# Two edits in a gated recurrence: the keys' transposes half a unit later, and the sums of squares as two split products

## The chip, the cores and the metric

The kernel runs on one core of a Trainium2 chip. The metric is the device time of one launch in microseconds (us). Three runs of the kernel before gave 2029.32, 2033.02 and 2034.14 us, so the median is 2033.02.

## The reference, cut to what matters

Two blocks follow each other, both on 1024 tokens of width 1024. The first one holds the stage that is changed: a recurrence of eight heads with 128 keys and 128 values each. Of one head it computes

```
z = h @ w_in                      # four of its parts: q, f_pre, i_in (the values v), g_h
f = lb + (1 - lb) * sigmoid(f_pre);   log_f = log(f);   k = 1 - f
o = recurrence(q, log_f, k, v)    # state <- decay * state + k_dec^T v, in chunks, causal
o = rms_norm(o, hgrn_norm_w) * silu(g_h)      # rms over the 128 values of the head
```

Everything is float32. Where the kernel needs float32 accuracy from TensorE it splits a matrix x into a rounded part hi (type fp32r) and the rest lo = x - hi, and adds the products of the parts.

## The kernel before, in words

**The stages.** After the first norm come the input projection with the recurrence, the pooling groups, the output projection, and then the second block. The recurrence lies between about 87 and 615 us of the profiled execution.

**The projection's units.** A unit is 128 columns of w_in over all tokens. A half unit (`fm_half`) is 8 x 3 matmuls of 128x512: for each k the three split products (lines 1003 to 1005). A head has four units, j = 0 for the forget gate, 1 for the output gate, 2 for the values, 3 for the queries. Units alternate between PSUM slots 0 and 1. The matmuls of unit 4 * it + j are for head it, while the tasks put between the half units are those of head h = it - 1. `head(h, z)` writes that order out by hand for TensorE:

```
z(0, 0)   task_o(h - 1)      z(0, 1)   task_ms(h - 1)
z(1, 0)   task_t0(h)   task_t1(h)      z(1, 1)   task_base(h)   task_span(h, 0)
z(2, 0)   task_span(h, 1)   task_u(h)  z(2, 1)   task_span(h, 2)
z(3, 0)   task_span(h, 3)    z(3, 1)   task_span(h, 4)
```

**The tasks.** `task_t0` (line 1131) transposes the values into PSUM slot 2 and `task_t1` (line 1140) the decayed keys into slot 3, eight transposes each. ScalarE copies both out (`take_vk`, through the copy helper at line 1693). `task_base` (line 1148, sixteen matmul records) multiplies keys and queries within blocks of 4. `task_span(h, j)` (line 1164) does it between the halves of blocks of 128, 64, 32, 16 and 8; spans 0 and 1 wait for the copied keys, since they write the banks of slot 3. `task_o` (lines 1181, 1183) makes the output of the head before in slot 3, and `task_ms` (line 1190) sums its squares over the partitions by a product with a matrix of ones, 128x512 for each half, into slot 2. Plain float32 matmuls show as two records each.

**ScalarE of a head** (`begin` and `step`): base exponentials (lines 1799, 1800), exponentials of spans 0 and 1 (line 1794), squares of the last output (line 1853), the exponential for the queries (line 1842), sigmoid of the forget gate (line 1807), `o_norm` with a Ln (line 1858) and an Exp (line 1860) that end in 1 / rms, then `take_vk`, the exponential of span 2, the output gate's sigmoid (line 1811), spans 3 and 4. An ACT_TABLE_LOAD stands ahead of most changes of function.

**VectorE of a head** (`spans`): base differences (lines 2562, 2565), differences of spans 0 and 1 (lines 2556, 2557), the products of keys and queries with the base exponentials (lines 2570, 2571), with those of span 0 (lines 2578, 2579), with the decayed queries (line 2632), then `back_3(h - 1)`, which waits for 1 / rms and scales the last head's output out of PSUM slot 3 (line 2656, after which `task_t1` may write that slot) and multiplies by the gate (line 2660), then the products of span 1, the differences of span 2, and the picks out of PSUM.

**GpSimd** rounds and splits the weights of each unit: line 795 makes w_hi, line 798 w_lo, 128x1024 each. The work for unit u starts when TensorE has finished unit u - 2 (the loop waits for `w_used` of 4 * i + s - 1). In four of the loop's turns it also makes sums of the output projection's weights (`t_sum_ahead`, line 822): one behind the first unit, one behind the second, two behind the third, none behind the fourth. SyncE's queue loads the weights ahead of all that.

Of the kernel before, what the change touches and what calls it, by code (L numbers as in the profile page):

```python
# [25 lines left out]
F32 = mybir.dt.float32  # L26
F32R = mybir.dt.float32r
I32 = mybir.dt.int32
ACT = mybir.ActivationFunctionType
ALU = mybir.AluOpType  # L30
# [190 lines left out]
def program(nc, ap):  # L221
    ctx = ExitStack()
    with ctx:
        def sb(name, shape, dt=F32):
            return ctx.enter_context(nc.sbuf_tensor(name, shape, dt))
# [15 lines left out]
        arena = sb("arena", [P, 27 * PAGE])  # L241
        arena_at = nc.sbuf_base - 27 * PAGE * 4
        ident = sb("ident", [P, P])
        ones = sb("ones", [P, P])
        cols = sb("cols", [P, VROWS])
        lvl_mask = sb("lvl_mask", [P, P + NL * 64], I32)
        st = sb("st", [P, 160])
# [10 lines left out]
        def page(i, n=1):  # L258
            return arena[:, i * PAGE:(i + n) * PAGE]
# [4 lines left out]
        def two_banks(slot):  # L264
            return psum[:, 2 * slot:2 * slot + 2, :].rearrange("p b n -> p (b n)")
# [53 lines left out]
        first_hi, first_lo = [first_[:, :, e, :] for e in range(2)]  # L319
        first_raw = page(FIRST_RAW, 2).rearrange("p (u c) -> p u c", c=PAGE)  # L320
        first_raw_k = lambda s: (first_raw if s < 2 else w_raw)[:, s, :].rearrange("p (k c) -> p k c", c=P)
        gate_part = [page(GATE_W)[:, h * HALF:(h + 1) * HALF] for h in range(2)]
        acc_mm = psum[:, X_BANKS, P:P + 2 * KT]
        gate_row = page(GATE_ROW)
# [672 lines left out]
        def _(pe):  # L997
# [127 lines left out]
            def task_t0(h):  # L1125

                pe.wait_ge(vt_done, h + 1)
                if not (type(h) is int and h == 0):
                    pe.wait_ge(ln_done, h)
                for i in range(NT):  # L1130
                    mm = pe.transpose(blocks128(two_banks(2), i), blocks128(page(B_VT), i), ident[:])
                mm.then_inc(task_full, 1)

            def task_t1(h):

                pe.wait_ge(kdec_done, h + 1)
                if not (type(h) is int and h == 0):
                    pe.wait_ge(o1_done, h)
                for i in range(NT):
                    mm = pe.transpose(blocks128(two_banks(3), i), blocks128(page(B_KDT), i), ident[:])  # L1140
                mm.then_inc(task_full, 1)
# [43 lines left out]

            def task_ms(h):

                pe.wait_ge(sq_done, h + 1)
                for half in range(2):
                    mm = pe.matmul(psum[:, 4 + half, :], ones[:], page(B_SQ)[:, half * HALF:(half + 1) * HALF], start=True, stop=True)  # L1190
                mm.then_inc(task_full, 1)

            def head(h, z):

                first = type(h) is int and h == 0
                z(0, 0)
                if not first:
                    task_o(h - 1)
                z(0, 1)
                if not first:  # L1200
                    task_ms(h - 1)
                z(1, 0)
                task_t0(h)
                task_t1(h)
                z(1, 1)
                task_base(h)
                task_span(h, 0)
                z(2, 0)
                task_span(h, 1)
                task_u(h)  # L1210
                z(2, 1)
                task_span(h, 2)
                z(3, 0)
                task_span(h, 3)
                z(3, 1)
                task_span(h, 4)
# [472 lines left out]
        def _(act):  # L1689
            A = act.activation  # L1690

            def copy(out, in_):
                return A(out, in_, ACT.Copy)  # L1693
# [98 lines left out]
            def span_exp(h, j):  # L1792
                act.wait_ge(d_done, NL * h + j + 1)
                A(page(B_D[j % 3]), page(B_D[j % 3]), ACT.Exp).then_inc(e_done, 1)

            def base_exp(h):

                act.wait_ge(d4_done, h + 1)
                A(page(B_K4), page(B_Q4), ACT.Exp, scale=-1.0).then_inc(e4_done, 1)
                A(page(B_Q4), page(B_Q4), ACT.Exp).then_inc(e4_done, 1)  # L1800
# [8 lines left out]
            def gate_sig(it):  # L1809
                act.wait_ge(w_used, 4 * it + 2)  # L1810
                A(mix_slot(it), two_banks(1), ACT.Sigmoid).then_inc(gsig_done, 1)
# [22 lines left out]
            def begin(h):  # L1834

                base_exp(h)
                span_exp(h, 0)
                span_exp(h, 1)
                if not (type(h) is int and h == 0):
                    o_squares(h - 1)  # L1840
                act.wait_ge(b_done, h + 1)
                A(qe, bB, ACT.Exp).then_inc(eb_done, 1)

            def take_vk(h):

                act.wait_ge(task_full, TASKS * h + 1)
                copy(page(B_V), two_banks(2)).then_inc(v_done, 1)
                act.wait_ge(task_full, TASKS * h + 2)
                copy(page(B_KD), two_banks(3)).then_inc(kd_done, 1)

            def o_squares(h):
                act.wait_ge(task_full, TASKS * h + TASK_O)
                A(page(B_SQ), two_banks(3), ACT.Square).then_inc(sq_done, 1)

            def o_norm(h):
# [17 lines left out]
            def step(it):  # L1873

                h = it - 1
                begin(h)
                front(it, 4 * it)
                if not (type(it) is int and it == 1):
                    o_norm(h - 1)
                take_vk(h)  # L1880
                span_exp(h, 2)
                gate_sig(it)
                span_exp(h, 3)
                span_exp(h, 4)
                take_v(it, 4 * it)
                log_f(it)
                take_q(it, 4 * it)
                decays(it)
# [6 lines left out]
            def pool_in(g, j):  # L1895
# [5 lines left out]
                else:  # L1901
# [5 lines left out]
            act.wait_ge(fc_done, HEADS)  # L1907
            pool_in(0, 0)
            o_norm(h - 1)
            take_vk(h)  # L1910
            act.dma_start(page(PW[0]).rearrange("p (g c d) -> p g c d", g=2, c=2),
                          ap["pool_w"][0, 0:2].rearrange("g (c p) d -> p g c d", p=P)).then_inc(pw_in, 16)
            span_exp(h, 2)
            pool_in(0, 1)
            span_exp(h, 3)
            span_exp(h, 4)
# [460 lines left out]
        def _(dve):  # L2377
# [186 lines left out]
                ref = page(B_K4)[:, 0:S // BASE].rearrange("p (n a) -> p n a", a=1).to_broadcast([P, S // BASE, BASE])  # L2564
                STT(x.rearrange("p (n w) -> p n w", w=BASE), ref, -0.5, b4, ALU.mult, ALU.add).then_inc(d4_done, 1)

            def base_kq(h):

                dve.wait_ge(e4_done, 2 * h + 2)
                TT(page(B_K4), page(B_K4), kk_, ALU.mult).then_inc(kq4_done, 1)  # L2570
                TT(page(B_Q4), page(B_Q4), qq, ALU.mult).then_inc(kq4_done, 1)

            def span_kq(h, j):
# [35 lines left out]
            def states(h):  # L2609
# [4 lines left out]
                for c in range(NT - 1):  # L2614
# [3 lines left out]
                    else:  # L2618
                        dve.wait_ge(s_done, (NT - 1) * h + c)
                        STT(sst[:, c * P:(c + 1) * P], sst[:, (c - 1) * P:c * P], end_decay[:, c:c + 1], u, ALU.mult, ALU.add).then_inc(s_done, 1)  # L2620

            def spans(h, gate, f):

                at = [(TASKS * h + SPAN_TASK[j], NL * h + j if j else h + 1) for j in range(NL)]
                base_d(h)
                span_d(h, 0)
                span_d(h, 1)
                dve.wait_ge(q_done, h + 1)
                base_kq(h)
                span_kq(h, 0)  # L2630
                dve.wait_ge(eb_done, h + 1)
                TT(qe, qe, qq, ALU.mult).then_inc(qe_done, 1)
                if not (type(h) is int and h == 0):
                    back_3(h - 1)
                span_kq(h, 1)
                span_d(h, 2)
                base_pick(h)
                span_kq(h, 2)
                pick(h, 0, at)
                span_d(h, 3)  # L2640
                gate()
                pick(h, 1, at)
                span_d(h, 4)
                states(h)
                span_kq(h, 3)
                span_kq(h, 4)
                pick(h, 2, at)
                f()
                pick(h, 3, at)
                pick(h, 4, at)  # L2650
# [41 lines left out]
            def window(g, c):  # L2692

                dve.wait_ge(pu_done, 2 * g + c + 1)
                u = page(U_PAGES[g % 2][c])
                src, w = u, 1
                for a in range(G_ORDER[g] + 1):
                    dst = page((S_A, S_B)[a % 2])
                    dve.tensor_copy(dst[:, 0:w], src[:, 0:w]).then_inc(win_step, 1)
                    steps[0] += 1  # L2700
                    wstep(TT(dst[:, w:S], src[:, w:S], src[:, 0:S - w], ALU.add))
                    src, w = dst, 2 * w
                dve.wait_ge(rc_in, 16)
                wstep(TT(src[:, 0:w], src[:, 0:w], page(RC)[:, 16 * G_ORDER[g]:16 * G_ORDER[g] + w], ALU.mult))
                TT(u[:, 0:w], src[:, 0:w], u[:, 0:w], ALU.subtract).then_inc(win_step, 1)
                steps[0] += 1
                STT(u[:, w:S], src[:, w:S], 1.0 / w, u[:, w:S], ALU.mult, ALU.subtract).then_inc(pd_done, 1)
                dve.wait_ge(pd_done, 2 * g + c + 1)
# [29 lines left out]
            spans(h, lambda: pool_gate(0, 0), lambda: pool_gate(0, 1))  # L2738
            dve.wait_ge(task_full, TASKS * h + TASK_O)
            window(0, 0)  # L2740
            window(0, 1)
            back_3(h)
            pool_gate(1, 0)
# [787 lines left out]
```

## Time and profile before

| | |
|---|---|
| median of three runs | 2033.02 us (2029.32 to 2034.14) |
| the profiled execution | 2031.16 us, of which the span is 2029.2 us |
| PE busy | 1973.9 us, 97% |
| DVE / ACT / POOL busy | 1352.0 (67%) / 824.5 (41%) / 941.1 us (46%) |
| the chain that ended last | PE 80%, DVE 10%, ACT 5%, issue 3% |
| mean granted TensorE clock | 0.992 of full speed |

PE is TensorE, DVE VectorE, ACT ScalarE, POOL GpSimd. The span runs from the first to the last instruction; the 2 us around it are the launch. The share of PE is an average over all stages. "Idle before" in a row is the time that the engine sat idle just before those instructions, with what ended it. Times in the timelines are microseconds from the start of the span: start, then duration. Matmuls overlap, so their cost in a stream is the distance from start to start.

### The profile page before, as it was taken

The page shows a single profiled execution, that of the slowest core. Times are in us where ns is not written, and L with a number is a line of the kernel's source. Part 1 is how long each engine was busy: PE and PEld are TensorE (multiplying, and loading weights), DVE is VectorE, ACT ScalarE, POOL GpSimd, SP SyncE. Part 2 cuts the span into 40 slices and gives each one's busy share as a digit, 9 for nine tenths or more (in the row PEclk, how much of TensorE's full clock was granted, in tenths as well). Part 3 has the DMA queues.
Part 4 walks back from the last instruction along what each step waited for, and adds up shares of the span by engine and source line. Part 5 has one row for each costly group of instructions (what it writes and reads, how often), then busy time and mean ns, then how long its engine had stood idle before and what let it go on. Part 6 is the DMA issues. An engine that isn't in the chain of part 4 may idle for free.

```text
span 2029.2 us, 27449 instructions
## 1 busy us (share of the span) xinstructions
PE 1973.9 (97%) x10053; PEld 1623.2 (80%) x10053; DVE 1352.0 (67%) x1784; ACT 824.5 (41%) x1313; POOL 941.1 (46%) x548
## 2 busy tenths in 40 slices
PE   7999999999999999999999899898999999999997
PEld 6888888888887768878888678776888888888886
DVE  7887777666536754687061487798856656667978
ACT  5444444344411014463200476657323323334443
POOL 1354454422324459753354110855755455445553
PEclk8999999999999999999999899999999999999999
DMA  9223222211122244044110200222423323357344
GB/s 285 75 81 117 73 72 103 84 40 31 42 63 58 68 156 135 11 177 126 42 51 11 84 2 1 73 104 80 139 88 109 114 88 109 103 183 242 104 137 164
DMA packets 179501, 193.98 MB, mean 96 GB/s; under 512 B 9863, under 2 KB 122968, under 8 KB 179418
## 3 DMA queue, kind: packets, MB, share of 16 engines
q1 hardware_dynamic: 172996, 178.53, 27.8%
q10 hardware_dynamic: 6422, 14.37, 2.0%
q8 instruction: 49, 0.80, 0.2%
q14 instruction: 34, 0.28, 0.0%
HBM read 151.71 MB, written 41.16 MB: 95 GB/s over the span
## 4 chain that ended last, share of the span: by engine, by line
PE 80%; DVE 10%; ACT 5%; issue 3%; POOL 1%; ACTq 0%; DVEq 0%; POOLq 0%
PE psum L1003 7%; PE psum L1558 7%; PE psum L1560 7%; PE psum L1559 7%; PE psum L1005 6%; PE psum L1004 6%; PE psum L1164 3%; PE psum L1661 3%; PE psum L1662 3%; PE psum L1663 3%; PE psum L1024 3%; PE psum L1025 3%; PE psum L1023 3%; PE psum L1319 2%; PE psum L1321 2%
## 5 line engine op out<-in xcount | busy, mean ns | idle before, releaser
L795 POOL TENSOR_TENSOR w_hi<-w_raw,ones 128x1024 fp32r<-128x1024 f32 x60 | 149.2, 2487 | 481.8 <-PE psum L1005 357.5
L1003 PE MATMUL psum<-h_hi,w_hi 128*128 128x512 f32 x704 | 284.2, 404 | 0.0
L1005 PE MATMUL psum<-h_hi,w_lo 128*128 128x512 f32 x704 | 274.8, 390 | 0.0
L1004 PE MATMUL psum<-h_lo,w_hi 128*128 128x512 f32 x704 | 274.2, 389 | 0.0
L798 POOL TENSOR_TENSOR w_lo<-w_raw,w_hi 128x1024 fp32r<-128x1024 f32 x60 | 166.7, 2779 | 4.7
L1693 ACT ACTIVATE arena<-psum 128x1024 f32<-128x1024 f32 (+7 forms) x103 | 80.3, 787 | 216.4 <-PE psum L1005 136.0
L1003 PEld LDWEIGHTS psum<-h_hi,w_hi 128*128 128x128 f32 x704 | 132.3, 188 | 28.5 <-issue 2.6
L1004 PEld LDWEIGHTS psum<-h_lo,w_hi 128*128 128x128 f32 x704 | 132.4, 188 | 28.3 <-issue 2.6
L1005 PEld LDWEIGHTS psum<-h_hi,w_lo 128*128 128x128 f32 x704 | 132.1, 188 | 28.4
L1661 PE MATMUL psum<-w_hi,h_hi 128*128 128x512 f32 x308 | 120.8, 392 | 3.1 <-DVE h_lo L3294 3.1
L993 POOL TENSOR_TENSOR w_lo<-arena,w_hi 128x512 fp32r<-128x512 f32 x61 | 86.3, 1419 | 75.5 <-ACT w_hi L1693 75.5
L1662 PE MATMUL psum<-w_lo,h_hi 128*128 128x512 f32 x308 | 120.5, 391 | 0.0
L1663 PE MATMUL psum<-w_hi,h_lo 128*128 128x512 f32 x308 | 120.4, 391 | 0.0
L1693 ACT ACTIVATE w_hi<-arena 128x512 fp32r<-128x512 f32 (+1 forms) x111 | 66.1, 605 | 83.7 <-DVE arena L3270 69.1
L1023 PE MATMUL psum<-w_hi,h_hi 128*128 128x512 f32 x256 | 99.6, 389 | 0.0
L1024 PE MATMUL psum<-w_lo,h_hi 128*128 128x512 f32 x256 | 99.6, 389 | 0.0
L1025 PE MATMUL psum<-w_hi,h_lo 128*128 128x512 f32 x256 | 99.6, 389 | 0.0
L1558 PE MATMUL psum<-h_hi,w_hi 128*128 128x512 f32 x252 | 98.2, 390 | 0.0
L1560 PE MATMUL psum<-h_hi,w_lo 128*128 128x512 f32 x252 | 98.1, 389 | 0.0
L1559 PE MATMUL psum<-h_lo,w_hi 128*128 128x512 f32 x252 | 98.0, 389 | 0.0
L984 POOL TENSOR_TENSOR w_lo<-w_raw,w_hi 128x512 fp32r<-128x512 f32 x40 | 64.6, 1616 | 63.2 <-ACT w_hi L1693 63.2
L3294 DVE TENSOR_TENSOR h_lo<-arena,h_hi 128x512 fp32r<-128x512 f32 x77 | 66.3, 867 | 35.3 <-ACT h_hi L1693 35.0
(489 smaller groups left out, 5227.5 us busy)
## 6 DMA issues: line engine op xcount, KB each, us to landing
w_raw<-w_in SPq DMA_DIRECT2D x64, 512.0 KB, 3.8
act_op<-arena SPq DMA_DIRECT2D x77, 256.0 KB, 2.3
arena<-act_op SPq DMA_DIRECT2D x77, 256.0 KB, 2.7
w_raw<-w_gate SPq DMA_DIRECT2D x22, 512.0 KB, 4.1
w_raw<-w_up SPq DMA_DIRECT2D x22, 512.0 KB, 5.2
arena<-ada_w SPq DMA_DIRECT2D x16, 512.0 KB, 7.2
arena<-w_out SPq DMA_DIRECT2D x16, 512.0 KB, 5.6
out_T<-arena SPq DMA_DIRECT2D x16, 512.0 KB, 5.8
```

Of the source, the lines that this page charges most:

```text
L798: pool.tensor_tensor(w_lo[:, c, :], raw, w_hi[:, c, :].bitcast(F32), ALU.subtract).then_inc(w_ready, 1)
L1003: pe.matmul(o, wh, xh, start=(k == 0), stop=False)
L1004: pe.matmul(o, wh, xl, start=False, stop=False)
L1005: return pe.matmul(o, wl, xh, start=False, stop=(k == KT - 1))
L1023: pe.matmul(psum[:, t, :], xh, wh, start=start, stop=False)
L1024: pe.matmul(psum[:, t, :], xh, wl, start=False, stop=False)
L1558: pe.matmul(o, wh[:, at], xh, start=(k == 0), stop=False)
L1559: pe.matmul(o, wh[:, at], xl, start=False, stop=False)
L1560: return pe.matmul(o, wl[:, at], xh, start=False, stop=(k == 3))
L1661: pe.matmul(o, ah, bh, start=(j == 0), stop=False)
L1662: pe.matmul(o, ah, bl, start=False, stop=False)
L1663: return pe.matmul(o, al, bh, start=False, stop=(j == DJ - 1))
```

## The change

It does three things. `task_t1` goes behind `z(1, 1)`, just ahead of `task_base`, on TensorE. ScalarE's `take_vk` is cut in two, and the copy of the keys goes behind the exponential of span 2. The sum of squares is split: ScalarE squares the output twice out of PSUM, once rounded to fp32r (page 5, one of the pages of the spans' differences) and once in full (page 7); VectorE subtracts one from the other in place; TensorE multiplies both with ones of type fp32r. ScalarE's squares go ahead of the exponentials of spans 0 and 1, and VectorE's subtraction between the two base products. No DMA changes its place, except that the load of the pooling weights in the last head stays behind the copy of the keys, and this copy is later.

```diff
-        ones = sb("ones", [P, P])
+        ones_r = sb("ones_r", [P, P], F32R)
+        ones = ones_r[:].bitcast(F32)
...
+        sq_hi, sq_lo = [rounded_pages(name, i, 1)[:] for name, i in (("sq_hi", B_D[2]), ("sq_lo", B_SQ))]
...
             def task_ms(h):
-                pe.wait_ge(sq_done, h + 1)
-                for half in range(2):
-                    mm = pe.matmul(psum[:, 4 + half, :], ones[:], page(B_SQ)[:, half * HALF:(half + 1) * HALF], start=True, stop=True)
+                for e, sq in enumerate((sq_hi, sq_lo)):
+                    pe.wait_ge(sq_done, 3 * h + (2 + e))
+                    for half in range(2):
+                        mm = pe.matmul(psum[:, 4 + half, :], ones_r[:], sq[:, half * HALF:(half + 1) * HALF], start=(e == 0), stop=(e == 1))
                 mm.then_inc(task_full, 1)
...
                 task_t0(h)
+                z(1, 1)
                 task_t1(h)
-                z(1, 1)
                 task_base(h)
...
             def begin(h):
                 base_exp(h)
+                if not (type(h) is int and h == 0):
+                    o_squares(h - 1)
                 span_exp(h, 0)
                 span_exp(h, 1)
-                if not (type(h) is int and h == 0):
-                    o_squares(h - 1)
...
             def o_squares(h):
                 act.wait_ge(task_full, TASKS * h + TASK_O)
+                A(sq_hi, two_banks(3), ACT.Square).then_inc(sq_done, 1)
                 A(page(B_SQ), two_banks(3), ACT.Square).then_inc(sq_done, 1)
...
-                take_vk(h)
+                take_vt(h)
                 span_exp(h, 2)
+                take_kd(h)
                 gate_sig(it)
...
+            def squares_lo(h):
+                dve.wait_ge(sq_done, 3 * h + 2)
+                TT(sq_lo, page(B_SQ), sq_hi.bitcast(F32), ALU.subtract).then_inc(sq_done, 1)
...
-                base_kq(h)
+                base_k(h)
+                if not (type(h) is int and h == 0):
+                    squares_lo(h - 1)
+                base_q(h)
                 span_kq(h, 0)
...
             window(0, 0)
+            squares_lo(h)
             window(0, 1)
```

`base_k` and `base_q` are the two instructions of `base_kq`. `take_vt` and `take_kd` are the two halves of `take_vk`, each with its own wait for TensorE.

## Rows read from the trace of the kernel before

**Rows 1.** The page's first part: busy time, share and instructions of each engine.
```profile
PE 1973.9 (97%) x10053; PEld 1623.2 (80%) x10053; DVE 1352.0 (67%) x1784; ACT 824.5 (41%) x1313; POOL 941.1 (46%) x548
```

**Rows 2.** PE's timeline in the fourth head: start, us, line, operation, count, idle before.
```profile
350.50 1.93 PE L1190 MATMUL psum<-arena,ones 128*128 128x512 f32 x4
...
357.76 1.03 PE L1131 MATMUL psum<-ident,arena 128*128 128x128 f32 x8
359.85 1.06 PE L1140 MATMUL psum<-ident,arena 128*128 128x128 f32 x8 [1.05 <-DVE arena L2656]
366.23 1.95 PE L1148 MATMUL psum<-arena 128*128 128x128 f32 x16
368.10 1.15 PE L1164 MATMUL psum<-arena 128*64 128x64 f32 x16
```

**Rows 3.** PE's timeline in the fifth head, where nothing waits.
```profile
414.21 1.88 PE L1190 MATMUL psum<-arena,ones 128*128 128x512 f32 x4
...
421.42 1.04 PE L1131 MATMUL psum<-ident,arena 128*128 128x128 f32 x8
422.29 1.04 PE L1140 MATMUL psum<-ident,arena 128*128 128x128 f32 x8
```

**Rows 4.** PE's timeline: fourth and last matmul of one half unit, twenty steps apart.
```profile
336.90 0.39 PE L1003 MATMUL psum<-h_hi,w_hi 128*128 128x512 f32 x1
...
341.43 0.39 PE L1005 MATMUL psum<-h_hi,w_lo 128*128 128x512 f32 x1
```

**Rows 5.** ACT's timeline in the fourth head.
```profile
349.39 1.01 ACT L1853 ACTIVATE arena<-psum 128x1024 f32<-128x1024 f32 x1
350.30 1.04 ACT L1842 ACTIVATE arena<-arena 128x1024 f32<-128x1024 f32 x1
...
365.33 1.06 ACT L1794 ACTIVATE arena<-arena 128x1024 f32<-128x1024 f32 x1 [3.35 <-DVE arena L2557]
```

**Rows 6.** DVE's timeline in the fourth head, and its line 2660 in the fifth.
```profile
351.37 3.38 DVE L2632 TENSOR_TENSOR arena<-arena 128x1024 f32<-128x1024 f32 x1
358.42 1.28 DVE L2656 SCALAR_TENSOR_TENSOR arena<-psum,cols,arena 128x1024 f32<-128x1024 f32 x1 [3.67 <-ACT arena L1860]
359.74 3.15 DVE L2660 TENSOR_TENSOR arena<-arena 128x1024 f32<-128x1024 f32 x1
...
364.62 0.68 DVE L2557 TENSOR_TENSOR arena<-arena 128x512 f32<-128x512 f32 x1
...
421.49 1.22 DVE L2660 TENSOR_TENSOR arena<-arena 128x1024 f32<-128x1024 f32 x1
```

**Rows 7.** POOL's timeline in the fourth head.
```profile
350.74 2.92 POOL L795 TENSOR_TENSOR w_hi<-w_raw,ones 128x1024 fp32r<-128x1024 f32 x1 [6.96 <-PE psum L1005]
...
356.97 4.83 POOL L822 TENSOR_TENSOR arena<-arena 128x1024 f32<-128x1024 f32 x2
366.47 2.35 POOL L795 TENSOR_TENSOR w_hi<-w_raw,ones 128x1024 fp32r<-128x1024 f32 x1 [4.66 <-PE psum L1005]
```

**Rows 8.** The timeline of POOL and DVE in the first head.
```profile
110.53 4.69 POOL L795 TENSOR_TENSOR w_hi<-w_raw,ones 128x1024 fp32r<-128x1024 f32 x1 [6.93 <-PE psum L1005]
...
115.29 2.72 POOL L798 TENSOR_TENSOR w_lo<-w_raw,w_hi 128x1024 fp32r<-128x1024 f32 x1
115.69 2.88 DVE L2579 TENSOR_TENSOR arena<-arena 128x512 f32<-128x512 f32 x1
```

**Rows 9.** The timeline of DVE and PE in the first head.
```profile
112.28 0.69 DVE L2557 TENSOR_TENSOR arena<-arena 128x512 f32<-128x512 f32 x1
...
113.28 1.15 PE L1164 MATMUL psum<-arena 128*64 128x64 f32 x16
```

**Rows 10.** PE's waits, 10 to 55 us: waited for, us in total, times, longest.
```profile
PE psum L1088 <- DVE arena L2467: 7.7, 1, 7.7
```

**Rows 11.** PE by microsecond at that wait: stretch, length, busy, granted clock.
```profile
32.00:33.00 1.00, 0.00 (x0) 0.58 1.18 288
...
39.00:40.00 1.00, 1.00 (x6) 1.00 1.19 298
```

More of the change, by code:

```diff
@@ L1836, in begin, with take_vt, take_kd @@
                 base_exp(h)
+                if not (type(h) is int and h == 0):
+                    o_squares(h - 1)
                 span_exp(h, 0)
                 span_exp(h, 1)
-                if not (type(h) is int and h == 0):
-                    o_squares(h - 1)
                 act.wait_ge(b_done, h + 1)
                 A(qe, bB, ACT.Exp).then_inc(eb_done, 1)
-            def take_vk(h):
+            def take_vt(h):
                 act.wait_ge(task_full, TASKS * h + 1)
                 copy(page(B_V), two_banks(2)).then_inc(v_done, 1)
+            def take_kd(h):
                 act.wait_ge(task_full, TASKS * h + 2)
@@ L1909, in _ @@
             o_norm(h - 1)
-            take_vk(h)
+            take_vt(h)
+            span_exp(h, 2)
+            take_kd(h)
             act.dma_start(page(PW[0]).rearrange("p (g c d) -> p g c d", g=2, c=2),
                           ap["pool_w"][0, 0:2].rearrange("g (c p) d -> p g c d", p=P)).then_inc(pw_in, 16)
-            span_exp(h, 2)
             pool_in(0, 1)
@@ L2565, in base_d, with base_k, base_q @@
                 STT(x.rearrange("p (n w) -> p n w", w=BASE), ref, -0.5, b4, ALU.mult, ALU.add).then_inc(d4_done, 1)
-            def base_kq(h):
+            def base_k(h):
                 dve.wait_ge(e4_done, 2 * h + 2)
                 TT(page(B_K4), page(B_K4), kk_, ALU.mult).then_inc(kq4_done, 1)
+            def base_q(h):
                 TT(page(B_Q4), page(B_Q4), qq, ALU.mult).then_inc(kq4_done, 1)
```

## The prediction

> **What bounds the kernel now.** I read the page first: TensorE is busy 97% of the span [rows 1], so an edit pays only where it shortens TensorE's stream or one of its few waits. Then the stream of one head. In the fourth head the values' transposes start at 357.76 and the keys' at 359.85 [rows 2]; undisturbed they are 0.87 apart [rows 3], so 1.22 us is lost, and the row blames VectorE's line 2656, which frees PSUM slot 3. Heads 1 to 4 show this wait (four rows alike), heads 5 to 7 none. The difference between them is GpSimd: in the fourth head it has two extra sums [rows 7], and VectorE's lines 2632 and 2660 stretch to 3.38 and 3.15 us, where line 2660 took 1.22 in the fifth head [rows 6]. They stretch because they wait for a GpSimd instruction to end: the two sums run from 356.97 to 361.80, and line 2660 ends at 362.89, one undisturbed length later. Line 2656, which reads PSUM, is not held (1.28).
>
> So the thing to follow is a chain beside TensorE: squares, 1 / rms, line 2656, line 2660, four half-page instructions, the exponential of span 2 at 365.33 [rows 5]. Today nothing on TensorE waits for that exponential before much later. After the change the keys' copy stands behind it on ScalarE, and `task_span(h, 0)` waits for that copy.
>
> **The change, part by part.**
>
> The products with ones. Today, in the fifth head, 7.21 us from their start to the next transposes [rows 3], less a half unit. Twenty steps of its matmuls take 4.53 us, 0.2265 each [rows 4], so 24 take 5.44 and the four float32 records 1.77. Four fp32r matmuls of the same width at 0.2265 are 0.91: 0.86 us less, in each of eight heads.
>
> The transposes. TensorE's work is the same; the wait of 1.22 goes from heads 1 to 4. What would be late next is the values' transposes, which wait for the Ln to leave slot 2, and then span 0.
>
> ScalarE. One more Square costs the distance between lines 1853 and 1842, 0.91 us [rows 5]. The squares lie ahead of everything up to 1 / rms, which moves from 358.4, where line 2656 waits for it [rows 6], to 359.3. The output is ready for them (`task_o` ends at 345). The copy of the keys, 1.03 us, moves behind the exponential.
>
> VectorE. The subtraction has the size of two half-page instructions, 1.2 us. It waits for the second square (349.45 by the shifted rows) and ends at 350.7, just before TensorE needs it after the two hi products (350.50 + 0.45): no wait there. VectorE then still has the base product of the queries, both span 0 products and line 2632 to do, 3.5 us, from 350.7 on. Until now only line 2632 was left at that moment.
>
> GpSimd's requests. Line 795 asks at 350.74 as before [rows 7], because z(0, 1) ends as before. Line 798 and the two sums follow, some 2.4 us each. The next line 795 asks when z(1, 1) ends. That was 366.23; now it is 357.0 (values' transposes, just held by the Ln) + 0.87 + 5.5 = 363.4, so it asks at 363.6 and not at 366.47. This is what the moved transposes trigger: two GpSimd instructions fall into the stretch in which VectorE has its last four short ones to do.
>
> How they share. At 115.69 a half-page VectorE instruction was issued while the one before it had itself been held; GpSimd, which had asked at 115.29, went first, and the VectorE one took 2.88 us for its 0.68 [rows 8]. So they alternate once both queue. The other bound is the first of these rows: GpSimd was kept for 2.3 us behind five VectorE instructions in a row that nothing had held (4.69 for 2.35). I work both out:
> - Alternating from 350.74: the queries' base product ends at 351.8, GpSimd 354.15, VectorE 354.75, GpSimd 357.1, VectorE 357.7, sum 360.05, line 2632 361.2, sum 363.55, line 2660 364.7 (line 2656 ran beside the sum), line 795 367.05, 367.65, line 798 370.0, then the last three short ones: 371.8.
> - VectorE first until it idles at 354.15: the four GpSimd instructions then run with line 2660 between the sums and the first short one behind them, and the chain ends at 371.95.
>
> Both end near 371.9, because from 350.7 on there are six GpSimd instructions (14.1) and VectorE's 7 us to fit in, with no hole left. Then come the exponential (1.06) and the copy (1.03): the keys are there at 374.1. TensorE, without that, would reach span 0 at 363.4 + 0.87 + 1.87 = 366.1. It stands 8.0 us, and span 0 starts 6.0 us later than the 368.10 of [rows 2]. This net already holds the two gains. Four heads: +24.0.
>
> The Trainium skill, page "SBUF — State Buffer", section "Who interferes with whom", says that a VectorE instruction with two SBUF inputs and a GpSimd one that reads SBUF exclude each other, the second to issue waiting out the first, and that one with at most one SBUF input is free. The rows of lines 2660 and 2656 agree with both halves. By the rule alone GpSimd would get in behind whatever VectorE runs when it asks, the first of my two orders; the row of 4.69 us bears out the second. The sum is the same to 0.2 us a head.
>
> The clock. TensorE has one long wait, 7.7 us [rows 10], from 27.5 to about 35.1. Before it the granted clock was full; it fell to half, 1.2 GHz, during the wait (0.58 between 32 and 33) and came back to 2.4 GHz only at 39 [rows 11]. Some 4.2 us of work ran at half speed: 2.1 us lost. A wait of 8.0 us should do the same. I take 2.1 for each of four: +8.4. The lower bound is 0; the upper is the whole half-clock stretch after the wait, about 6.8 us and so 3.4 lost.
>
> The first head. It has no squares. The base products there wait for the copied values anyway. VectorE's difference for span 2 ends at 112.97 [rows 9]; exponential and copy end at 115.1, and span 0 follows instead of 113.28: +1.8. If line 795 came first there, it would be +4.2.
>
> The later heads, 5 to 7. There is no extra sum. In the fifth head line 2660 starts at 421.49 now [rows 6] and, with the later 1 / rms, at 422.3 then; VectorE's short ones end 3.6 us later at 425.9, the exponential at 427.0. The keys' transposes end at 427.8 (421.42 - 0.86 + 0.87 + 5.5 + 0.87), so the copy waits for them and is done at 429.05, before TensorE's 429.7. Only the products' gain stays: three times 0.86, and once more for the eighth head's products during the pooling stage, where VectorE has the subtraction done long before: -3.4.
>
> The sum against the profiled execution's 2031.16: +24.0 + 8.4 + 1.8 - 3.4 = +30.8, so 2062.0. The median of the runs is 1.9 above that execution, within their spread of 4.8, and I leave it there. Everything behind the recurrence is again TensorE's and moves along.
>
> **The rivals.**
> 1. Only one GpSimd instruction gets between the short ones. Span 0 is then 3.5 us late, not 6.0 or 6.1: 2031.2 + 14.0 + 1.8 - 3.4 = 2043.6, or up to 2052 with the clock. For it: an unheld VectorE run kept GpSimd out once [rows 8]. Against: the run would have to begin unheld.
> 2. VectorE keeps its run together: the four short ones end at 367.0, the keys are there at 369.2, +1.1 a head: 2031.2 + 4.6 + 1.8 - 3.4 = 2034.2, no change that can be told.
> 3. The other side: the chain keeps ahead of TensorE in all heads, as in 5 to 7. Then 8 x 0.86 + 4 x 1.22 = 11.8 comes off: 2019.4. This decides where the keys are copied by 366.1. Unheld all the way, the chain would give 359.3 + 1.3 + 3.6 + 2.1 = 366.3, so it needs GpSimd to stay out of the way. For it: in the later heads the same chain is in time, and the order in which the two engines meet is worked out from shifts of tenths of a microsecond. Against: 14.1 us of GpSimd work has nowhere to go in that stretch.
> 4. The clock stays at half for longer, or the subtraction comes after line 795's request (its margin is 0.05 us) and holds the products with ones for about 3 us as well: up to 2074.
>
> **How the numbers follow.** My case has 0.42, rival 1 has 0.20, rival 2 has 0.13, rival 3 has 0.15, rival 4 has 0.10. The number is my case's, 2062.0; its own range, with the clock's bounds, is 2053 to 2068. With rivals 1 and 2 taken in, the range is 2032 to 2068; left out are the third and most of the fourth. A difference of 0.3%, 6 us, is about what a measurement of this kernel can tell from none: faster 0.15, within it 0.13, slower 0.72.
>
> **What would show it.** Right: in heads 1 to 4 the span 0 row of PE has an idle time of about 8 us released by ScalarE's copy; the second short instruction of line 2578 or 2579 before it takes about 2.9 us; the granted clock has four dips; the products with ones are four records at 0.23 apart; heads 5 to 7 show no wait. Wrong: no idle time before span 0 in the loop's first turns, or one of 1 us; or a wait before the products with ones.

## The result and the profile after

The changed kernel takes 2059.69 us (median of 4 runs, 2057.79 to 2060.74) against 2033.58 us: a ratio of 1.0134, with a 95% interval of 1.0122 to 1.0147. The profiled execution took 2059.16 us, 28.0 more than that of before. The forecast was 2062.0.

The page's first part, and the list of PE's longest wait in the recurrence (waited for, us in total, times, longest):

```profile
PE 1978.0 (96%) x10053; PEld 1631.9 (79%) x10053; DVE 1384.9 (67%) x1792; ACT 831.6 (40%) x1321; POOL 954.4 (46%) x548
```
```profile
PE psum L1166 <- ACT arena L1696: 28.3, 5, 6.7
```

Against [rows 1] TensorE's busy time grew by 4.1 us and its idle time in the span by 24.0. The idle time lies in five waits of span 0 (now line 1166) for ScalarE's copy, 28.3 us in all, where the kernel before had four waits of 1.05. Line numbers have moved. On TensorE 1133 and 1142 are the two transposes, 1150 the base products, 1193 the products with ones. On ScalarE 1696 is the copy and 1797 the spans' exponential. On VectorE 2636 is the subtraction, 2583 the queries' base product, 2590 and 2591 the spans' products, 2651 the decayed queries' product, 2675 and 2679 the old 2656 and 2660, and 2565 and 2566 the spans' differences. On GpSimd 797, 800 and 824 are the old 795, 798 and 822. PE's timeline in the fourth head, to be held against [rows 2]:

```profile
373.73 0.61 PE L1193 MATMUL psum<-sq_hi,ones_r 128*128 128x512 f32 x2
374.18 0.62 PE L1193 MATMUL psum<-sq_lo,ones_r 128*128 128x512 f32 x2
...
380.30 1.06 PE L1133 MATMUL psum<-ident,arena 128*128 128x128 f32 x8
386.69 1.04 PE L1142 MATMUL psum<-ident,arena 128*128 128x128 f32 x8
387.56 1.95 PE L1150 MATMUL psum<-arena 128*128 128x128 f32 x16
396.16 1.97 PE L1166 MATMUL psum<-arena 128*64 128x64 f32 x16 [6.64 <-ACT arena L1696]
```

Both intended gains are there. The products with ones take 0.90 us (the next half unit starts at 374.63), and the keys' transposes follow z(1, 1) with no wait. Then TensorE stands for 6.64 us, and the 16 records behind it take 1.97 us where they took 1.15: the granted clock is 0.50 from 395 to 401. ScalarE's timeline shows what came last:

```profile
394.06 1.06 ACT L1797 ACTIVATE arena<-arena 128x1024 f32<-128x1024 f32 x1 [10.61 <-DVE arena L2566]
395.02 1.01 ACT L1696 ACTIVATE arena<-psum 128x1024 f32<-128x1024 f32 x1
```

The keys' transposes were done at 387.7, but their copy stood behind an exponential that waited until 394.06 for VectorE. VectorE's timeline, with GpSimd's under it, shows why, against [rows 6, 7]:

```profile
372.67 1.23 DVE L2636 TENSOR_TENSOR sq_lo<-arena,sq_hi 128x1024 fp32r<-128x1024 f32 x1 [0.35 <-ACT arena L1860]
373.81 1.22 DVE L2583 TENSOR_TENSOR arena<-arena 128x1024 f32<-128x1024 f32 x1
374.94 2.90 DVE L2590 TENSOR_TENSOR arena<-arena 128x512 f32<-128x512 f32 x1
377.76 2.88 DVE L2591 TENSOR_TENSOR arena<-arena 128x512 f32<-128x512 f32 x1
380.56 3.41 DVE L2651 TENSOR_TENSOR arena<-arena 128x1024 f32<-128x1024 f32 x1
383.90 1.27 DVE L2675 SCALAR_TENSOR_TENSOR arena<-psum,cols,arena 128x1024 f32<-128x1024 f32 x1
385.20 2.11 DVE L2679 TENSOR_TENSOR arena<-arena 128x1024 f32<-128x1024 f32 x1
387.24 2.84 DVE L2590 TENSOR_TENSOR arena<-arena 128x512 f32<-128x512 f32 x1
390.00 2.82 DVE L2591 TENSOR_TENSOR arena<-arena 128x512 f32<-128x512 f32 x1
```
```profile
373.97 3.32 POOL L797 TENSOR_TENSOR w_hi<-w_raw,ones_r 128x1024 fp32r<-128x1024 f32 x1 [6.95 <-PE psum L1007]
377.37 2.72 POOL L800 TENSOR_TENSOR w_lo<-w_raw,w_hi 128x1024 fp32r<-128x1024 f32 x1
380.05 6.18 POOL L824 TENSOR_TENSOR arena<-arena 128x1024 f32<-128x1024 f32 x2
386.93 2.60 POOL L797 TENSOR_TENSOR w_hi<-w_raw,ones_r 128x1024 fp32r<-128x1024 f32 x1 [0.70 <-PE psum L1007]
389.61 2.67 POOL L800 TENSOR_TENSOR w_lo<-w_raw,w_hi 128x1024 fp32r<-128x1024 f32 x1
```

A half-page instruction of 0.68 us takes 2.8 to 2.9 in four places, each time with one GpSimd instruction inside, and lines 2651 and 2679 are held in the same way by the two sums; six GpSimd instructions lie between 373.97 and 392.28. Line 2675, which reads PSUM, is not held. In the fifth head, without the sums, nothing waits:

```profile
457.19 1.04 PE L1142 MATMUL psum<-ident,arena 128*128 128x128 f32 x8
458.06 1.95 PE L1150 MATMUL psum<-arena 128*128 128x128 f32 x16
459.94 1.15 PE L1166 MATMUL psum<-arena 128*64 128x64 f32 x16
```

The granted clock around the four waits, 25 us each (stretch, length, PE busy, clock, then the DMA's share and rate):

```profile
180.00:205.00 25.00, 21.35 (x117) 0.81 0.52 190
251.00:276.00 25.00, 21.16 (x115) 0.80 0.53 189
322.00:347.00 25.00, 20.74 (x120) 0.86 0.53 189
392.00:417.00 25.00, 20.84 (x116) 0.86 0.25 68
```

The clock has two levels here, full (2.4 GHz) and half (1.2 GHz), so 0.81 of 25 us means some 9.5 us at 1.2 GHz and 0.86 some 7, a part of it inside the wait.

### The profile page after: what moved, and what is told of

It reads as the page before. It is cut to its first block, busy times and chain, and to the rows that moved or that the text cites. A ratio compares the mean times of both kernels' runs of the same rounds, so it can differ in the third digit from the quotient of the medians.

```text
span 2057.3 us, 27477 instructions
## 1 busy us (share of the span) xinstructions
PE 1978.0 (96%) x10053; PEld 1631.9 (79%) x10053; DVE 1384.9 (67%) x1792; ACT 831.6 (40%) x1321; POOL 954.4 (46%) x548
## 4 chain that ended last, share of the span: by engine, by line
PE 78%; DVE 13%; ACT 4%; issue 3%; POOL 1%; ACTq 0%; DVEq 0%; POOLq 0%
PE psum L1561 6%; PE psum L1562 6%; PE psum L1563 6%; PE psum L1005 6%; PE psum L1007 6%; PE psum L1006 6%; PE psum L1166 3%; PE psum L1664 3%; PE psum L1666 3%; PE psum L1665 3%; PE psum L1026 3%; PE psum L1025 3%; PE psum L1027 3%; PE psum L1322 2%; PE psum L1324 2%
## 5 line engine op out<-in xcount | busy, mean ns | idle before, releaser
L797 POOL TENSOR_TENSOR w_hi<-w_raw,ones_r 128x1024 fp32r<-128x1024 f32 x60 | 156.2, 2603 | 497.2 <-PE psum L1007 373.0
L1166 PE MATMUL psum<-arena 128*128 128x64 f32 (+1 forms) x640 | 73.0, 271 | 28.3 <-ACT arena L1696 28.3
L1166 PEld LDWEIGHTS psum<-arena 128*128 128x128 f32 (+1 forms) x640 | 73.2, 189 | 32.1 <-issue 27.3
```

The lines of the kernel that those rows point to most:

```text
L1166: mm = pe.matmul(o, kq[:, 0:rows], late, start=True, stop=True)
```

## The experiments

Ten kernels, in three groups in the order below: four, four and two. The ones of a group ran on one chip, with the kernel before beside them (medians 2030.16, 2032.96 and 2032.79 us), so ratios are to that. "The port" in the expectations is what VectorE's instructions with two SBUF inputs and GpSimd's share, so that one holds the other.

**The copy put back ahead of the exponential.** In the loop and in the last head:

```diff
                 take_vt(h)
-                span_exp(h, 2)
                 take_kd(h)
+                span_exp(h, 2)
```

> The changed kernel with one swap on ScalarE: the copy of the keys goes back ahead of the exponential of span 2. Theory (the wait before span 0 comes from the copy standing behind an exponential that VectorE feeds late): the keys are there about 1.2 us after their transposes end, before the base products end, so the wait of 6.6 us and the four clock dips go away; both intended gains appear, 8 x 0.86 and 4 x 1.22 us: about 2031.2 - 11.8 = 2019 to 2022 us, faster than both kernels. Rival (the chain of VectorE and GpSimd decides whatever ScalarE's order is): the wait moves to another task of the same heads, span 1 or span 2 or the products with queries, and the time stays at 2045 or more. Second rival (the exponential of span 2 is now what is late): a wait of 1 to 4 us before span 2 in heads 1 to 4, 2025 to 2035.

Measured: 2020.77 us, ratio 0.9950 (0.9935 to 0.9964), faster than both kernels. PE's only wait between 95 and 660 us is one that the kernel before had too, in the first head:

```profile
PE psum L1150 <- ACT arena L1696: 0.9, 1, 0.9
```

So the whole loss came through the place of that one copy, and both rivals fall. The chain beside TensorE is as late as it was: the exponential of span 2 starts 20.39 us behind the head's products with ones (365.92 against 345.53), in the changed kernel 20.33. But nothing that TensorE needs soon stands behind it, and the wait did not move to span 1 or 2.

**The transposes alone.** The changed kernel with the sums of squares as before (one Square behind the exponentials of spans 0 and 1, float32 products, no subtraction).

> Only the keys' transposes and their copy moved, sums of squares as before. Theory: GpSimd's next request comes at 364.4 on the clock of the kernel before, when VectorE is already in its unheld run of four short instructions (362.8 to 365.3) and keeps the port; the exponential ends at 366.4, the copy at 367.4, span 0 starts 0.6 us earlier than before in heads 1 to 4 after an idle time of about 0.6 us, too short for the clock to fall; first head +1.8 us. Sum about -0.6: 2030 to 2034 us. Rival (the moved transposes alone bring the collision): two GpSimd instructions in between, span 0 starts 4 us late, 2045 to 2055 us.

Measured: 2047.11 us (2040.17 to 2049.99), ratio 1.0082 (1.0065 to 1.0099). The theory was wrong here. The rival had the sign and the range, but with two GpSimd instructions in between, and there is one. In the profiled execution, of 2040.17 us, span 0 waits 2.7 us in each of the four heads. The rows of DVE and POOL:

```profile
370.23 0.68 DVE L2562 TENSOR_TENSOR arena<-arena 128x512 f32<-128x512 f32 x1
...
370.83 2.84 DVE L2563 TENSOR_TENSOR arena<-arena 128x512 f32<-128x512 f32 x1
```
```profile
370.53 2.59 POOL L796 TENSOR_TENSOR w_hi<-w_raw,ones 128x1024 fp32r<-128x1024 f32 x1 [2.50 <-PE psum L1006]
```

VectorE was in its third short instruction of an unheld run, and GpSimd went in ahead of the fourth. I had expected the run to keep GpSimd out. One GpSimd instruction in between is 2.2 us, so the first three heads took 65.2 us each and not 63.1. The fourth took 66.8, and there alone the granted clock fell behind the wait:

```profile
375.00:400.00 25.00, 24.20 (x134) 0.93 0.25 66
```

So after a wait of 2.7 us the clock fell in one head of this execution and not in the three before, at a price of 1.6 us. The three executions of 2046 to 2050 us had a lower mean clock (0.986 to 0.988) than the profiled one (0.990). It is an estimate that it fell in more of their heads: 0.003 of 2047 us is 6 us of clock, about 12 us at the lower level, which cost 6 us. That is most of the difference.

**The squares alone.** Transposes side by side again, both copies ahead of the exponential of span 2, squares split.

> Only the sums of squares split; the transposes of values and keys stand together and both copies ahead of the exponential of span 2, as before. Theory: in heads 1 to 4 VectorE comes to line 2656 of the kernel before some 2 to 3.5 us later, because the subtraction pushes three instructions behind GpSimd's request and they alternate; the keys' transposes wait for it 3 to 5 us instead of 1.2. The products save 0.86 in each of eight heads. Sum: 4 x (2 to 3.5) - 6.9 = +1 to +7: 2032 to 2040 us. Rival (the subtraction is hidden, the squares are harmless): 2031.2 - 6.9 + 4 x 0.9 (1 / rms later by a Square) = 2028 us.

Measured: 2047.69 us, ratio 1.0086 (1.0066 to 1.0105): worse than the theory's range. The wait before the keys' transposes is as expected, the granted clock behind it is not. The waits of the loop and the row of the fourth head:

```profile
PE psum L1142 <- DVE arena L2675: 17.1, 6, 3.9
```
```profile
376.41 1.94 PE L1142 MATMUL psum<-ident,arena 128*128 128x128 f32 x8 [3.91 <-DVE arena L2675]
```

Eight transposes take 1.94 us instead of 1.04: half the clock, in each of the four heads (mean clock 0.88 to 0.90 in 25 us there). I had left the clock out of that sum. A head took 68.4 us for 63.7: 2.85 more of waiting, 0.87 less of products, and the 2.7 that are left fit the clock (0.10 to 0.12 of 25 us is 2.5 to 3.0). The four heads make 18.7 us, and the profiled execution (2047.54) is 16.4 above 2031.16; the rest of the program took 2.3 less.

**The two sums moved.** The changed kernel with

```diff
-                    for name in (["T3"], ["T2"], ["T1", "T4"], [])[s]:
+                    for name in (["T3"], ["T2"], [], ["T1", "T4"])[s]:
```

> The changed kernel, with GpSimd's two sums of a loop turn behind the fourth unit instead of the third, so that they are not in the queue between the products with ones and span 0. Theory (the port between VectorE and GpSimd makes the chain late): VectorE's instructions wait for 2 GpSimd instructions fewer, span 0 of heads 1 to 4 starts about 4 to 5 us earlier, an idle time of 0 to 3 us is left, and the clock mostly stays full: 2031 to 2042 us. Rival (the extra Square, the subtraction and the copy's new place make the chain late without GpSimd): no change against the changed kernel, 2055 to 2060 us.

Measured: 2023.49 us, ratio 0.9964 (0.9950 to 0.9977). All four waits are gone; only the first head's, 1.7 us, is left:

```profile
PE psum L1166 <- ACT arena L1696: 1.7, 1, 1.7
```

This took more off than I had expected. With two GpSimd instructions in the first group and not four, VectorE began its last short instruction at 360.93 on that execution's clock, just ahead of GpSimd's next request at 361.03. So it is not two instructions that drop out but four: the second group falls behind the whole run, by a margin of 0.1 us. Nothing was changed on ScalarE, so the extra Square and the copy's new place are harmless once GpSimd's instructions are out of the way.

**The same move in the kernel before (control).**

> The kernel before, with GpSimd's two sums of a loop turn behind the fourth unit instead of the third. Control for the runs that move these sums. Theory (the wait of 1.2 us before the keys' transposes in heads 1 to 4 comes from VectorE being held by GpSimd's instructions ahead of line 2656): it goes away, 4 x 1.2 us: about 2025 to 2027 us. Rival (it comes from ScalarE's chain to 1 / rms alone): no change.

Measured: 2031.64 us, ratio 0.9997 (0.9987 to 1.0006): no change. The wait before the keys' transposes stays as in [rows 2]:

```profile
PE psum L1140 <- DVE arena L2656: 4.2, 4, 1.1
```

So the gain above is not one of moving the sums as such. And the theory was wrong on where that wait comes from; a later run settles it. [rows 6] could have told as much: behind line 2632 VectorE sits idle for 3.67 us until ScalarE's 1 / rms is there, so the hold of line 2632 delays nothing, and line 2660 comes behind line 2656.

**The squares alone, with the sums moved.**

> Only the sums of squares split, and the sums behind the fourth unit. Theory (the loss of the squares alone, 3.9 us of waiting before the keys' transposes and the half clock behind it, comes from the port and not from the extra Square): 1 / rms is 0.9 us later than in the kernel before, so a wait of 0.5 to 1.5 us before the keys' transposes is left in up to seven heads, and 0.86 comes off in eight: 2022 to 2028 us. Rival (the subtraction and the Square are too long by themselves): the wait stays above 3 us and the time above 2040.

Measured: 2035.43 us, ratio 1.0016 (1.0007 to 1.0026). Between the two statements. The four long waits fall from 3.9 to 2.6 us, not to 0.5 to 1.5:

```profile
PE psum L1142 <- DVE arena L2675: 11.9, 6, 2.6
```

What is left is, by my estimate, the 1.05 us of before, 0.9 from the second Square and 0.86 because TensorE arrives sooner by the shorter products, 2.8 in all; I had left the last out. The 1.3 us that went are the share of the two sums. The granted clock fell behind the first of these waits (eight transposes in 1.94 us) and not behind the other three (1.06 us).

**The transposes alone, with the copy ahead.**

> Only the keys' transposes moved, with the copy of the keys ahead of the exponential of span 2. Theory: the wait of 1.2 us in heads 1 to 4 is all that the move can save, 4.9 us: 2025 to 2027 us, so the split products account for the other 5 to 7 us of the 2020.8 of the version with both. Rival (the move by itself also lets GpSimd start earlier and shortens more): 2021 to 2023 us, and the split products give next to nothing.

Measured: 2026.70 us, ratio 0.9974 (0.9964 to 0.9983). Heads 1 to 6 take 62.4 us each. This is as expected, and it splits the gain: 5 to 6 us for the move, and the rest of the 10 us of the version with both for the products with ones. In the profiled executions the last products with ones start at 612.27 us before, 606.99 with the move and 602.78 with both. From there to the end the three take 1416.9, 1416.7 and 1415.8 us.

**The wait filled.** The changed kernel with work thrown away in heads 1 to 6:

```diff
                 task_base(h)
+                if type(h) is not int:
+                    pe.wait_ge(sig_done, h + 2)
+                    for _ in range(28):
+                        pe.matmul(psum[:, 0, :], ones_r[:], h_hi[:, 0, 0:HALF], start=True, stop=True)
                 task_span(h, 0)
```

> The changed kernel, with 28 matmuls of ones by a slice of h_hi (128x512, fp32r, 6.3 us, into a PSUM slot whose content has been taken) between the base products and span 0 in the loop's heads 1 to 6. They only keep TensorE busy; their product is thrown away. Theory (the half clock behind the wait costs TensorE 1.7 to 3.4 us in each of heads 1 to 4): span 0 starts at the same distance from the head's start as without them, the granted clock stays full there, and each of heads 1 to 4 gets shorter by 2 to 3.5 us (70.7 us from one products with ones to the next becomes 67.5 to 69); heads 5 and 6 get 6 us longer. Sum: 2059 - 8 to -14 + 12 = 2057 to 2063 us. Rival (the clock costs nothing, the wait is all): heads 1 to 4 keep 70.7 us, 2070 us.

Measured: 2062.48 us, ratio 1.0146 (1.0130 to 1.0163). PE's timeline in the fourth head, and the granted clock there:

```profile
381.66 1.95 PE L1150 MATMUL psum<-arena 128*128 128x128 f32 x16
383.37 6.60 PE L1213 MATMUL psum<-h_hi,ones_r 128*128 128x512 f32 x28
```
```profile
387.00:412.00 25.00, 24.63 (x144) 1.00 0.24 63
```

The clock stays full in all four. The slow heads take 68.6 us each (299.25 to 367.83 between products with ones) instead of 71.2, 71.4, 69.9 and 70.8: 1.3 to 2.8 us less, 2.2 on average, at the same distance from base products to span 0 (8.67 against 8.60). Two heads are longer by 6.4. So the half clock behind the wait is worth 2.2 us a head on average, and the rival falls.

**The single sum moved, kernel before.** The order is now `(["T3"], [], ["T2"], ["T1", "T4"])`: the single sum goes behind the third unit, and the two of the third behind the fourth, which alone had changed nothing.

> The kernel before, with the single sum that stands behind the second unit put behind the third, and the two of the third behind the fourth. Moving the two alone left the wait before the keys' transposes as it was. Theory (that wait comes from the single sum: it holds VectorE's base differences for 2.2 us in heads 1 to 4, so that the whole chain to 1 / rms is 2.2 us later than in heads 5 to 7): the wait of 1.2 us goes away in the four heads, 62.4 us a head instead of 63.7, about 2031 - 5 = 2026 us. Rival (something else in these turns holds it, the transfers of the sums' operands for example): 63.7 us a head stay.

Measured: 2026.38 us, ratio 0.9971 (0.9960 to 0.9981). The wait is gone, and a head takes 62.4 us. DVE's line 2562 in the fourth head, first in the kernel before, then in this one:

```profile
341.50 2.79 DVE L2562 TENSOR_TENSOR arena<-arena 128x256 f32<-128x256 f32 x1
```
```profile
338.35 0.60 DVE L2562 TENSOR_TENSOR arena<-arena 128x256 f32<-128x256 f32 x1
```

PE's two groups of transposes stand 0.87 apart:

```profile
354.56 1.03 PE L1131 MATMUL psum<-ident,arena 128*128 128x128 f32 x8
355.43 1.04 PE L1140 MATMUL psum<-ident,arena 128*128 128x128 f32 x8
```

The 1.2 us were lost some 15 us ahead of where the wait shows (341.50 to 344.29, against 358.80).

**No subtraction.** The changed kernel without `squares_lo` and the lo product; its sums are those of the rounded squares alone.

> The changed kernel without VectorE's subtraction and without the product of the lo part (the sums of squares are those of the rounded squares alone); both Squares stay on ScalarE. Theory (the number of GpSimd instructions that come between decides, and they stay six): worked out from the changed kernel's rows, the last short instruction ends 0.6 us earlier, TensorE comes to span 0 0.46 us earlier, so the wait there stays at 6.0 to 6.6 us in heads 1 to 4; with 8 x 0.45 us of products less the time is 2053 to 2057 us. Rival (the subtraction is what makes the chain late, since without it and the second Square the wait was 2.7 us): 3 to 4.5 us of waiting, about 2042 to 2048 us.

Measured: 2052.63 us, ratio 1.0096 (1.0079 to 1.0112). The waits of the loop:

```profile
PE psum L1166 <- ACT arena L1696: 24.1, 5, 5.6
PE psum L1133 <- ACT arena L1865: 2.1, 4, 0.5
```

Span 0 waits 5.6 us a head, a little under the 6.0 to 6.6 expected and well above the rival's, and the values' transposes now wait 0.5 for the Ln. So the subtraction is not what makes the loss. But the run does not show that the number six decides either. GpSimd's second group falls ahead of the third and fourth short instruction, not the first and second, and VectorE is held five times, not six. The first of the two sums runs mostly while VectorE stands still and waits for 1 / rms:

```profile
378.94 1.28 DVE L2673 SCALAR_TENSOR_TENSOR arena<-psum,cols,arena 128x1024 f32<-128x1024 f32 x1 [2.10 <-ACT arena L1867]
380.26 2.40 DVE L2677 TENSOR_TENSOR arena<-arena 128x1024 f32<-128x1024 f32 x1
```

Lines 2673 and 2677 are 2675 and 2679 of the changed kernel. Here the chain is set by ScalarE up to 1 / rms, and behind it by three GpSimd instructions, one of which holds line 2677 and two of which hold the last short ones.

## Why the prediction was right, and where it was off

The time, the sign and the mechanism came out as forecast; two of the steps came out wrong without moving the sum. By the prediction's steps:

**The products with ones.** Forecast 0.86 us a head; in heads without waits 61.5 us against 62.4, 0.87. Right.

**The wait of 1.22 us.** It went, as forecast. Its cause was put wrongly: the text held it against lines 2632 and 2660 and the two sums. Moving these two changed nothing; moving the single sum away from behind the second unit removed it. That sum holds line 2562, the base differences, for 2.2 us, and the whole chain to 1 / rms starts later. The number was right because it was read off the two kinds of head.

**GpSimd's requests and the sharing.** Forecast: requests at 350.74 and 363.6, six instructions in between, VectorE done at 371.8. On the clock of the fourth head before (23.2 us earlier than the rows above), they came at 350.7 and 363.7, and VectorE was done at 370.8. TensorE was ready at 366.3, forecast 366.1, and span 0 started at 372.9, forecast 374.1. The wait was therefore 6.64 us and not 8.0: the term was too large by 1.36 us a head, 5.4 in all. The sequence was the first of the two that I worked out, and each instruction is held by the one I named; but every meeting was costed 0.1 to 0.2 us too long: I took GpSimd's full 2.35 us beside VectorE's 0.6, 2.95 from one short instruction to the next, and the rows show 2.82 (374.94 to 377.76). The six meetings make 1.0 of the 1.2 us by which span 0 came sooner than forecast. The fourth rival gave the subtraction a margin of 0.05 us against GpSimd's request, counted from its end. In these rows GpSimd gets in behind the VectorE instruction that runs when it asks, so the start counts: 372.67 against 373.97, a margin of 1.3 us. The rule of the Trainium skill, page "SBUF — State Buffer", section "Who interferes with whom", is what these rows show: two SBUF inputs are held, a PSUM input is not.

**The second bound, VectorE keeping its run.** It was drawn from one row, in the first head. In the fourth it did not hold, as the run with the transposes alone shows. In the first head it held in every version. In the forecast it changed the sum by 0.2 us a head; in the expectation of that run it was taken for the rule, and 2.2 us a head were missed.

**The clock.** Forecast 2.1 us a head from the one long wait of before [rows 10, 11]; the filled wait shows 2.2 on average. Right in size. The upper bound was read wrongly: the 6.8 us at half clock in [rows 11] begin inside the wait, and only 3.9 of them lie behind it (35.1 to 39.0). The clock also falls after waits of 3.9 us every time and of 2.7 us sometimes, which I had not counted on.

**The first head and the later ones.** +1.8 forecast. Its wait is 1.67 us, and span 0 moves from 113.28 [rows 9] to 115.14. Heads 5 to 7 show no wait and are shorter by 0.87 each: right.

**The sum.** Four slow heads grew from 63.7 to 71.2, 71.4, 69.9 and 70.8, together 28.4 us; forecast 32.4. With 1.9 up to the first of them and 2.6 taken off in heads 5 to 7, the last products with ones start 27.7 us later than before (639.94 against 612.27). What follows takes 1417.4 us against 1416.9, so the saving forecast for the eighth products can't be told from what executions differ by (the control, whose products are unchanged, takes 1415.6). The rivals: the first two had fewer GpSimd instructions in between than the rows show. Of the fourth, nothing waits before the products with ones; the half clock did last some 10 us in two of the heads, against 6.8 in [rows 11], but on average it cost the 2.2 us. The time of the third (the chain keeps ahead) is what both the copy put back and the moved sums come near to, 2020.8 and 2023.5 against its 2019.4. It is not the change that was wrong but one line of its order.

## What to carry to other kernels

Where an engine's queue is strict, ask of every moved step what it stands behind now: a copy that TensorE needs in 2 us was put behind an exponential fed by VectorE, which GpSimd holds up, and the place of that one line turned a gain of some 10 us into a loss of 26 to 28. When TensorE gets faster or its order changes, the requests that its progress releases on GpSimd move too; count the instructions that VectorE must let in between, not the shares of busy time, and look where it stands still anyway. And give a wait of several microseconds on TensorE a second price, the lower clock behind it. The releaser that a wait names can be the last link of a longer chain: the 1.2 us of the kernel before came from a hold some 15 us earlier on another engine.

## What the runs showed of the hardware

GpSimd and VectorE share in two ways that the runs tell apart but don't explain. In the loop's heads a GpSimd instruction gets in behind the VectorE instruction that runs when it asks: in the run with the transposes alone it asked at 370.53, during an instruction that ended at 370.91, and held the next one for 2.2 us. In the first head it was kept until the end of VectorE's unheld run, three to four more instructions, in the traces of all twelve kernels: 4.7 to 5.6 us for 2.35 (5.57 in the changed kernel, 4.69 in [rows 8]), ending 2.2 us after VectorE's run did. What differs there is open.

The granted clock fell in each of four heads after waits of 3.9, 5.6 and 6.6 us, and after waits of 2.6 to 2.7 us in one of four, in two profiled executions; after waits of 1.05 us it stayed full. 28 matmuls in the gap kept it full. Executions of one kernel with such waits differ by up to 10 us (2040.17 to 2049.99) where the four versions without a wait in heads 1 to 7 differ by 2.9 to 3.6 (2019.93 to 2023.56 the widest).
